# A delta-rule recurrence: two preparation stages and two chunk stages become two round stages, and the late modulation moves from TensorE to ScalarE and GpSimd

## The reference, cut to what matters

```python
mod = jax.nn.silu(c) @ ada_w + ada_b          # 6 x 1024 values; the last 4 x 1024 are "late"
...
w_log = -jax.nn.softplus(-(w0 + jnp.tanh(wd) @ w_decay_up)) - 0.5
decay = jnp.exp(-jnp.exp(w_log))
a = jax.nn.sigmoid(a0 + ad @ w_aaa_up)
kk = (k * k_k) per head, divided by its norm
k = k * (1 + (a - 1) * k_a)
def step(S, inp):
    r_t, w_t, k_t, v_t, a_t, b_t = inp        # a_t = -kk, b_t = kk * a
    sa = jnp.einsum('bhij,bhj->bhi', S, a_t)
    S = S * w_t[:, :, None, :] + sa[..., None] * b_t[:, :, None, :] + v_t[..., None] * k_t[:, :, None, :]
    return S, jnp.einsum('bhij,bhj->bhi', S, r_t)
```

## Time and profile before

| What | us |
|---|---|
| median of three runs | 2764.87 |
| the profiled execution, whole | 2762.08 |
| its span, first to last instruction | 2759.1 |
| TensorE busy in the span | 2668.9 (97%) |
| VectorE busy | 1884.4 (68%) |
| ScalarE busy | 1205.4 (44%) |
| GpSimd busy | 285.1 (10%) |
| mean granted TensorE clock | 0.985 |

### The profile page before, as it was taken

One profiled execution on the slowest core, in us unless ns is written; L12 is line 12 of the kernel. 1 busy time (PEld: TensorE's weight loads), 2 busy tenths in 40 slices (PEclk: granted clock), 3 DMA queues, 4 the chain that ended last, 5 costly groups with the idle time before them and its releaser, 6 DMA issues. The chain is left out here.

```text
span 2759.1 us, 48978 instructions
## 1 busy us (share of the span) xinstructions
PE 2668.9 (97%) x19134; PEld 2281.0 (83%) x19134; DVE 1884.4 (68%) x3427; ACT 1205.4 (44%) x2294; POOL 285.1 (10%) x217
## 2 busy tenths in 40 slices
PE   7988899999999999999999999999999999999998
PEld 5868766778888789998878999989999857899997
DVE  3454668552332588887457888888888767788885
ACT  3232235531212454445256544465444438654444
POOL 2000114422111300001401000010000100100000
PEclk9999889999999999999999999999999999999999
DMA  8250310123232223334303333332333331323331
GB/s 279 63 169 16 111 38 5 62 77 107 92 95 88 77 77 97 110 92 124 92 17 92 89 104 96 104 107 86 109 99 101 83 86 26 92 79 113 92 108 54
DMA packets 369540, 248.89 MB, mean 90 GB/s; under 512 B 28692, under 2 KB 364376, under 8 KB 369312
## 3 DMA queue, kind: packets, MB, share of 16 engines
q1 hardware_dynamic: 368818, 245.18, 30.2%
q10 hardware_dynamic: 494, 0.59, 0.1%
HBM read 241.52 MB, written 2.12 MB: 88 GB/s over the span
## 5 line engine op out<-in xcount | busy, mean ns | idle before, releaser
L3018 ACT CAST dense_wt_hi<-ring 128x512 fp32r<-128x512 f32 x719 | 444.4, 621 | 462.5 <-PE bank L3068 220.5
L3023 DVE TENSOR_TENSOR dense_wt_lo<-ring,dense_wt_hi 128x512 fp32r<-128x512 f32 x719 | 493.6, 689 | 105.8 <-ACT dense_wt_hi L3018 104.4
L3055 PE MATMUL bank<-dense_operand_hi,dense_wt_hi 128*128 128x256 f32 x1248 | 353.7, 283 | 4.2 <-DVE h L3672 4.2
L3057 PE MATMUL bank<-dense_operand_hi,dense_wt_lo 128*128 128x256 f32 x1248 | 353.1, 283 | 0.0
L3056 PE MATMUL bank<-dense_operand_lo,dense_wt_hi 128*128 128x256 f32 x1248 | 353.1, 283 | 0.0
L3068 PE MATMUL bank<-dense_act_hi,dense_wt_hi 128*128 128x512 f32 x832 | 258.4, 392 | 0.8 <-DVE dense_act_lo L3336 0.8
L3068 PE MATMUL bank<-dense_act_lo,dense_wt_hi 128*128 128x512 f32 x832 | 257.1, 390 | 0.0
L3068 PE MATMUL bank<-dense_act_hi,dense_wt_lo 128*128 128x512 f32 x832 | 256.7, 390 | 0.0
L3055 PE MATMUL bank<-feat_hi,dense_wt_hi 128*128 128x256 f32 (+1 forms) x820 | 246.8, 301 | 7.5 <-DVE h L3707 3.2
L3055 PEld LDWEIGHTS bank<-dense_operand_hi,dense_wt_hi 128*128 128x128 f32 x1248 | 238.8, 191 | 12.2 <-issue 5.0
L3057 PE MATMUL bank<-feat_hi,dense_wt_lo 128*128 128x256 f32 (+1 forms) x820 | 245.8, 300 | 0.0
(11 more groups left out here) (726 smaller groups left out, 5429.3 us busy)
## 6 DMA issues: line engine op xcount, KB each, us to landing
ring<-in_ffn_w_up SPq DMA_DIRECT2D x88, 512.0 KB, 3.9
ring<-in_ffn_w_gate SPq DMA_DIRECT2D x88, 512.0 KB, 5.2
ring<-in_ffn_w_down SPq DMA_DIRECT2D x60, 512.0 KB, 4.8
ring<-in_ada_w SPq DMA_DIRECT2D x24, 1024.0 KB, 8.0
ring<-in_ffn_w_down SPq DMA_DIRECT2D x52, 256.0 KB, 3.9
ring<-in_w_ffn_gate SPq DMA_DIRECT2D x11, 1024.0 KB, 5.3
ring<-in_w_ffn_up SPq DMA_DIRECT2D x11, 1024.0 KB, 5.4
ring<-in_w_in SPq DMA_DIRECT2D x8, 1024.0 KB, 6.5
```

What stands on the lines that cost most here:

```text
L3018: self.nc.scalar.copy(self.hi(i), src).then_inc(self.s_high, 1)
L3023: self.nc.vector.tensor_tensor(self.lo(i), self.items[i][1], self.hi(i).bitcast(F32), ALU.subtract).then_inc(self.s_low, 1)
L3055: pe.matmul(out, h[:, w], xh, start=start and k == 0, stop=False, skip_group_check=shared)
L3057: last = pe.matmul(out, l[:, w], xh, start=False, stop=stop and k == 3, skip_group_check=shared)
```

## The change

The two stages of a round become one, `rwkv_round_stage`, and within it:

1. Before the steps begin only `A` and `B` are made. `RT`, the chunk ends, `BH`, the scaled key `K` and `KH` are made by VectorE between the evacuations of the steps (`receptance`, `ends`, `scaled_key`, `last_key`). Steps that read them wait on `s_late`. GpSimd no longer makes `KH` and `BH`; they come from `B` and `K` and the chunk ends.
2. The exponentials are three per group instead of four, with the scale folded in; two VectorE operations on the log decay per group go.
3. The tanh of `wa` and the load of the small weights `wl` move into `in_proj_stage`; a table load for the root stands at the head of the round.
4. The transposed values `vt` are made before the steps (50 steps instead of 52), and the extra steps stand in another order; one place in the second level is empty.
5. The late modulation: ScalarE multiplies a ring tile by `c` in place (8 operations of 128x256 a tile), GpSimd adds the eight pieces in three operations (128x1024, 128x512, 128x256), and TensorE turns the 8 sums into columns after the last step, before the state steps. ScalarE takes two tiles each behind steps 3, 7, 15 and 25.

```diff
+    def scale(self, act, r):
+        K.wait_loaded(act, n)
+        for k in range(KD):
+            last = self.nc.scalar.mul(w[:, k, :], w[:, k, :], K.coef[:, k:k + 1])
+        last.then_inc(self.s_scaled, 1)
+    def add(self, pool, r):
+        pool.wait_ge(self.s_scaled, r + 1)
+        t(w[:, 0:4 * WC], w[:, 0:4 * WC], w[:, 4 * WC:8 * WC], ALU.add)
+        pool.drain()
+        t(w[:, 0:2 * WC], w[:, 0:2 * WC], w[:, 2 * WC:4 * WC], ALU.add)
+        pool.drain()
+        t(self.acc[:, r, :], w[:, 0:WC], w[:, WC:2 * WC], ALU.add).then_inc(self.s_acc, 1)
+        pool.drain().then_inc(K.tiles_done, 1)
+    def turn(self, pe):
+        for r in range(self.count):
+            pe.wait_ge(self.s_acc, r + 1)
+            for m in range(2):
+                last = pe.matmul(K.bank[self.turned][:, at:at + 1], self.acc[:, r, m * P:(m + 1) * P], K.k("ones")[:, 0:1], ...)
...
@@ in_proj_stage
+        if t == len(tiles) - 2:
+            e.wait_ge(box["read"], t)
+            nc.scalar.activation(M.wa[0:64, :], M.wa[0:64, :], ACT.Tanh)
...
@@ tensor, before the steps
-                mod.begin(pe)
-                mod.chunk(pe, at)
...
-                for r in range(at + 3, at + 8):
-                    mod.chunk(pe, r)
-                mod.turn(pe, at + 7)
+                for e in range(2):
+                    for out, l, r, start, stop in full(e, value(e), None, 2):
+                        last = pe.matmul(out, l, r, start=start, stop=stop)
+                    last.then_inc(s_v, 1)
+                pe.wait_ge(s_sig, 4)
+                K.keep_clock(pe, K.bank[0], 8)
...
@@ vector
+                for e in range(2):
+                    dve.wait_ge(s_exp, 2 * e + 1)
+                    v.tensor_tensor(W[e].A, W[e].at, W[e].T, ALU.mult)
+                    dve.wait_ge(s_exp, 2 * e + 2)
+                    v.tensor_tensor(W[e].B, W[e].B, W[e].rk, ALU.mult).then_inc(s_ready, 1)
+                def receptance(e):
+                    v.tensor_tensor(W[e].RT, M.rkv[:, ps[e], :], W[e].kht, ALU.mult).then_inc(s_late, 1)
+                def ends(e):
+                    v.tensor_copy(R.end[:, e, :], chunks(W[e].kht)[:, :, C - 1])
+                    v.tensor_scalar(W[e].akt, W[e].bht, K.p("k_a", ps[e]), oka[:, e:e + 1], ALU.mult, ALU.add)
+                    v.tensor_tensor(chunks(W[e].BH), chunks(W[e].B), end(e), ALU.mult).then_inc(s_late, 1)
+                def scaled_key(e):
+                    v.tensor_tensor(key(e), key(e), W[e].akt, ALU.mult)
+                    v.tensor_tensor(W[e].K, key(e), W[e].rk, ALU.mult).then_inc(s_late, 1)
+                def last_key(e):
+                    v.tensor_tensor(chunks(W[e].KH), chunks(W[e].K), end(e), ALU.mult).then_inc(s_late, 1)
+                receptance(0)
...
+                    if n == 1:
+                        receptance(1)
+                    elif n in (3, 5):
+                        ends((n - 3) // 2)
+                    elif n in (9, 13):
+                        scaled_key((n - 9) // 4)
+                    elif n in (17, 19):
+                        last_key((n - 17) // 2)
...
@@ scalar, behind step n
+                    if n in (3, 7, 15, 25):
+                        for r in range(2):
+                            mod.scale(act, (3, 7, 15, 25).index(n) * 2 + r)
```

More of the change, by code:

```diff
@@ L2627, in _ @@
             def _(pool):
-                pool.wait_ge(s_pe, n_A)
-                for e in range(2):
-                    nc.gpsimd.tensor_tensor(chunks(R.W[e].A), wide("eye"), R.end[:, e, :].unsqueeze(2).broadcast_to([P, NCH, C]),
-                                            ALU.mult).then_inc(s_diag, 1)
+                for r in range(mod.count):
+                    if r == 6:
+                        pool.wait_ge(s_pe, n_A)
+                        for e in range(2):
+                            nc.gpsimd.tensor_tensor(chunks(W[e].A), wide("eye"), end(e), ALU.mult).then_inc(s_diag, 1)
+                    mod.add(pool, r)
@@ L2633, in _ @@
             @block.vector
             def _(dve):
-                for n, (g, _, evacs) in enumerate(steps):
+                for e, p in enumerate(ps):
+                    v.tensor_scalar(W[e].at, key(e), K.p("k_k", p), None, ALU.mult).then_inc(s_kk, 1)
+                for e, p in enumerate(ps):
+                    v.tensor_scalar(oka[:, e:e + 1], K.p("k_a", p), -1.0, 1.0, ALU.mult, ALU.add)
+                    v.memset(chunks(W[e].T)[:, :, 0:1], 1.0)
+                for e in range(2):
+                    dve.wait_ge(s_root, e + 1)
+                    v.tensor_scalar(root[:, e, :], root[:, e, :], 1e-12, None, ALU.max)
+                    dve.drain()
+                    v.reciprocal(root[:, e, :], root[:, e, :]).then_inc(s_inv, 1)
@@ new lines, in _ @@
+                for e in range(2):
+                    dve.wait_ge(s_spread, e + 1)
+                    v.scalar_tensor_tensor(W[e].at, W[e].at, -1.0, K.bank[4 * e + 3][:, :], ALU.mult, ALU.mult)
+                for e in range(2):
+                    dve.wait_ge(s_sig, e + 1)
+                    v.tensor_tensor_scan(W[e].kht, K.k("reset"), W[e].vt, 0.0, ALU.mult, ALU.add).then_inc(s_scan, 1)
+                dve.drain()
+                for e in range(2):
+                    dve.wait_ge(s_sig, 3 + e)
+                    v.scalar_tensor_tensor(W[e].B, W[e].at, -1.0, W[e].bht, ALU.mult, ALU.mult)
@@ new lines, in _ @@
+                dve.drain()
+                for e in range(2):
+                    dve.wait_ge(s_exp, 2 * e + 1)
[3 more added lines that the diff above has]
+                def receptance(e):
+                    dve.wait_ge(s_grow, e + 1)
+                    v.tensor_tensor(W[e].RT, M.rkv[:, ps[e], :], W[e].kht, ALU.mult).then_inc(s_late, 1)
@@ new lines, in _ @@
+                for e in range(2):
+                    act.wait_ge(s_kk, e + 1)
+                    a.activation(W[e].akt, W[e].at, ACT.Square).then_inc(s_sq, 1)
+                for e in range(2):
+                    act.wait_ge(s_norm, e + 1)
+                    a.activation(root[:, e, :], K.bank[4 * e + 3][:, 0:8], ACT.Sqrt).then_inc(s_root, 1)
+                for e, p in enumerate(ps):
+                    act.wait_ge(s_lora, 2 * e + 1)
+                    a.activation(W[e].vt, K.bank[4 * e][:, :], ACT.Sigmoid, bias=K.p("w0", p)).then_inc(s_sig, 1)
@@ new lines, in _ @@
+                for e, p in enumerate(ps):
+                    act.wait_ge(s_lora, 2 * e + 2)
+                    a.activation(W[e].bht, K.bank[4 * e + 1][:, :], ACT.Sigmoid, bias=K.p("a0", p)).then_inc(s_sig, 1)
+                for e in range(2):
+                    act.wait_ge(s_scan, e + 1)
+                    a.activation(chunks(W[e].T)[:, :, 1:C], chunks(W[e].kht)[:, :, 0:C - 1], ACT.Exp, scale=NEG_SQRT_E).then_inc(s_exp, 1)
+                    a.activation(W[e].rk, W[e].kht, ACT.Exp, scale=-NEG_SQRT_E).then_inc(s_exp, 1)
@@ new lines, in _ @@
+                for e in range(2):
+                    act.drain()
+                    a.activation(W[e].kht, W[e].kht, ACT.Exp, scale=NEG_SQRT_E).then_inc(s_grow, 1)
+                for e in range(2):
+                    act.wait_ge(s_v, e + 1)
+                    a.copy(W[e].vt, K.bank[4 * e + 2][:, :]).then_inc(s_vt, 1)
+                if rnd == 0:
+                    a.activation(M.g[:, :], M.g[:, :], ACT.Sigmoid)
+                    a.activation(M.g2[:, :], M.g2[:, :], ACT.Sigmoid)
@@ L2661, in _ @@
+                for n, (g, _, evacs, _) in enumerate(steps):
                     if n_act[n]:
```

311 lines of the change are left out of this document (126 added, 185 removed).

## The result

The changed kernel takes 2774.18 us (median of eight runs, 2764.39 to 2778.13) against 2762.11 of the kernel before in the same sessions: a ratio of 1.0041, 95% interval 1.0029 to 1.0054, so slower by some 11 us. The prediction said 2746 and is wrong: in size by 28 us, and in sign. The profiled execution took 2771.09, its span 2769.2 against 2759.1.

What follows compares the result with a forecast made beforehand. The head was taken as bound by a chain through all engines, the steps by TensorE with VectorE close behind. Terms -15.2 + 0 + 3.3 + 3.2 + 0.3 = -8.4 a round, -16.8 in all, gave 2746 us, range 2736 to 2758.

Steps and rivals of the forecast that it cites:

- Heads: Stretch of each round before TensorE's first 64x64 step: 13.9 us instead of 29.2, so -15.2 a round.
- Steps without collision: Inversion steps of a round, if GpSimd's adds disturb nothing: even with before, taken as 0.
- The terms 1.5 - 2.6 + 1.3: In the steps: step 12 later by 1.5 us, second level shorter by 2.6, third level paying back 1.3.
- Collisions: In the steps, GpSimd's adds slow VectorE's operations with two SBUF inputs: 3.3 us a round, a third of the bound.
- bound of 9.6: In the steps, all nine two-input VectorE operations slowed by 1.07 us each, all on the path: 9.6 us a round.
- about 22: Sign in the steps that VectorE is slowed by GpSimd: step 12 about 22 us behind step 0.
- Rival 2: In the steps, a long GpSimd add holds VectorE until it ends: about 10 us a round, 2759 in all; chance 0.15.
- The row of 1.75: Profile row in the old head: a two-input VectorE product took 1.75 us instead of 0.68 while GpSimd ran.
- rival 3: In the steps, TensorE's waits lower its clock; 16 unhidden steps cost 13 us a round, 2771 in all; chance 0.06.
- signs of being wrong: Head over 17 us, granted clock near 0.5 for over 15 us of a round's steps, or turning products waiting for GpSimd.
- Ends: Behind the steps, each round: turning products +3.2 us and column sums on VectorE +0.3.
- Scaling on ScalarE: In the steps, 16 scalings per two tiles take 5 us, fitting before the next copy: cost 0.

Runs made afterwards that it cites:

- version with nothing else at the end: Changed kernel with late modulation on TensorE between steps, no GpSimd adds, plus 16 unread turning products behind each round's last step: 2754.81 us, ratio 0.9974.
- first late version: Changed kernel, but GpSimd's first add of a round waits until TensorE has passed its 20th step: 2776.18 us, ratio 1.0055.

## Why the prediction was wrong

**Heads: right.** 13.4 and 13.4 us against 13.9. The table loads took 1.28 us each and cost nothing that the row did not say. By the 2.66 us of the Trainium skill, page "ScalarE: Activation LUTs", section "What ACT_TABLE_LOAD costs", the head would have been some 2 us longer than forecast (an estimate); the trace disagrees with it.

**Steps without collision: right.** Said even with before, 66.2; the run without adds has 65.4 and 66.7. (The terms 1.5 - 2.6 + 1.3 add up to +0.2, not to -0.2, which changes nothing; and step 12 came at 19.2 there, not at 20.3.)

**Collisions: the step that failed.** "I take 3.3, a third" of a bound of 9.6. The stretch was 9.4 and 9.6, and the steps grew by 12.6 and 14.4 with the adds. That the stretch meets the bound of 9.6 is luck: two things were wrong in the working. The price of a hit is not 1.07 but what is left of GpSimd's instruction, from 0.3 to 2.1 in the eight of the nine operations that were hit in round 0, and the short copies of chunk ends (0.16 alone, 0.42 and 0.76 here) are held too. And the two thirds that were taken as hidden were not: step 12 stood at 26.0 us instead of the "about 22" of the prediction. With TensorE's gaps filled the same stretch costs 2.7 and 3.1, so cover is possible, but this kernel had none. Rival 2 named the mechanism and the price, 10 us a round, and had a chance of 0.15. The Trainium skill, page "SBUF — State Buffer", section "Who interferes with whom", says that who issues first has the shared pair for the whole instruction, and that a VectorE instruction with at most one SBUF input does not contend outside the two-port modes. For products, sums and transposes all runs agree: 2.62 behind an add of 2.35, 0.98 behind adds of about 0.8, 0.69 and 0.71 for PSUM sums and transposes throughout. Two forms with one SBUF input were held all the same: the copy of 128x8 (0.16 alone, up to 1.77) and, in the run of short adds only, a scaled sigmoid (0.54 alone, twice 1.02). In which mode they ran no trace says. The row of 1.75 could not tell a held VectorE from a slowed one, since GpSimd's products beside it, at 1.72, were as long as itself.

**The clock: a rival's term that came on top.** The sum had nothing for it, and rival 3 was to decide by itself from 16 unhidden steps. It came with the collisions: of the 12.6 and 14.4 us, 3 to 5 a round go with the clock, by either division above. I had taken the two as alternatives; but with the adds the clock was 0.91 and 0.87, without them 1.00 and 0.97. One of the prediction's own signs of being wrong came true by it: 0.87 over the 81.1 us of round 1 are some 21 us at half clock (an estimate from that row), more than its 15. Rival 3's 2771 is close to the measured 2774 by luck, since the larger part of the loss was waiting for VectorE.

**Ends: mis-sized.** Predicted +3.5 a round, measured +4.6 and +5.1. The products took 4.29 (4.2 predicted), but the state steps behind them took 5.9 instead of 4.5. In the version with nothing else at the end they cost 8.4 to 11.0 us over both rounds; the prediction had 6.4.

**Scaling on ScalarE: its duration was off, its cost right.** 16 scalings took 6.5 us, not 5, and cost nothing where the tile was loaded. In the first late version this same queue cost 9.6 us a round. "Ring tiles come free later than before, but a load has more than 10 us to spare" thus held for the changed kernel, and not once the adds were late.

The sum over both rounds of the profiled execution: -16.8 predicted; steps +19.6 (8.5 and 11.1 over the predicted 69.5 and 70.0), ends +2.7, heads -1.1, and the unchanged stages +5.7, which makes the +10.1 of the span.

## What to carry to other kernels

Before work goes to GpSimd, list what VectorE does in that time that reads two SBUF tiles: each can wait for the whole of the running GpSimd instruction, so place the long ones beside VectorE's PSUM work (-17.4 us here) or cut them short (-17.5). The price depends on what TensorE does meanwhile: with its waits filled by real work the same stretch of VectorE cost 3 us a round instead of 12.6 to 14.4. And a delayed queue hands its lateness on: each late version had to be followed to the next instruction behind it, first on ScalarE, then on GpSimd.

## What the runs showed of the hardware that was not expected

- GpSimd's copy of 128x1024 takes 1.12 us on average, its add 2.35 to 2.57, and the copy holds VectorE too.
- GpSimd is held as well: its add of 512 columns took 1.53 next to VectorE's two-input work and 1.26 to 1.28 beside PSUM work.
- A busy TensorE can lose its clock: behind 32 records of one column the granted clock was 0.50 with no idle time ahead, and the state steps took 5.9 us instead of 4.5.
- The clock fell in the steps of the version without any late modulation (0.59 and 0.53) and not in round 0 of the one without adds, though TensorE waited for VectorE equally long in both.
- TensorE can stop for up to 2.7 us in the middle of a step, just behind the load of a ring tile; the cause is not shown.
